# Attention scores of the second and third mixer as three products of high and low parts, with keys, queries and values projected in that order

## The reference

```python
def _diff_attention(dq, dk, dv, lam):
    s = jnp.einsum('bqhjd,bkhjd->bhjqk', dq, dk).astype(jnp.float32) * ATTN_SCALE
    p = jax.nn.softmax(s, axis=-1)
    a = (p[:, :, 0] - lam * p[:, :, 1]).astype(dv.dtype)
    return jnp.einsum('bhqk,bkhe->bqhe', a, dv)

def _gqa_attention(gq, gk, gv):
    s = jnp.einsum('bqhgd,bkhd->bhgqk', gq, gk).astype(jnp.float32) * ATTN_SCALE
    p = jax.nn.softmax(s, axis=-1).astype(gv.dtype)
    return jnp.einsum('bhgqk,bkhd->bqhgd', p, gv)
...
    dq, dk = _apply_rope(dq, cos, sin), _apply_rope(dk, cos, sin)
    gq, gk = _apply_rope(gq, cos, sin), _apply_rope(gk, cos, sin)
```

## Time and profile before

| | |
|---|---|
| median of three runs | 4403.17 us (4396.05 to 4407.77) |
| the profiled execution | 4407.63 us |
| its span | 4405.6 us |
| TensorE busy | 3956.6 us (90%) |
| VectorE, ScalarE, GpSimd busy | 2291.0, 1369.2, 1346.1 us |
| d of mix2, 1498 to 1616 us | granted clock 0.91 |
| g of mix2, 1838 to 1975 us | granted clock 0.99 |
| d of mix3, 3278 to 3372 us | granted clock 0.94 |
| g of mix3, 3538 to 3652 us | granted clock 0.97 |

### The profile page before, as it was taken

How to read it: one execution, slowest core, us unless ns; L and a number is a source line. 1 busy time by engine, 2 the same in 40 slices (tenths; PEclk the granted TensorE clock), 3 DMA queues, 4 the chain that set the end, 5 groups by cost and what they waited for, 6 DMA issues and landing times.

```text
span 4405.6 us, 50811 instructions
## 1 busy us (share of the span) xinstructions
PE 3956.6 (90%) x18628; PEld 3175.8 (72%) x18628; DVE 2291.0 (52%) x3495; ACT 1369.2 (31%) x1832; POOL 1346.1 (31%) x1012
## 2 busy tenths in 40 slices
PE   7999899989997979789879879999787989788999
PEld 6888676867776748558668768888674747577887
DVE  4676844146664361641682367777445353834334
ACT  3222633242224242252112331111424243225223
POOL 2444332434432103003222223322220303434443
PEclk8999999999998989899989989999998999899999
DMA  4454221233331102001111123332110201222222
GB/s 180 176 190 156 85 72 63 96 115 128 137 132 49 39 0 72 20 1 58 57 58 58 58 82 125 118 119 100 45 48 10 82 1 67 77 84 79 95 95 86
DMA packets 57219, 364.66 MB, mean 83 GB/s; under 512 B 5744, under 2 KB 12144, under 8 KB 13936
## 3 DMA queue, kind: packets, MB, share of 16 engines
q1 hardware_dynamic: 42064, 271.11, 17.5%
q10 hardware_dynamic: 15008, 91.49, 5.5%
HBM read 360.49 MB, written 2.10 MB: 82 GB/s over the span
## 4 chain that ended last, share of the span: by engine, by line
issue 66%; POOL 23%; PE 10%; DVE 0%; ACT 0%; POOLq 0%; DVEq 0%; ACTq 0%
POOL b_wlo L561 23%; PE ps L1647 3%; PE ps L1648 3%; PE ps L1649 3%; POOLq L575 0%; ACT ps L616 0%; DVE b_y L1156 0%; DVE b_x L1160 0%; PE ps L1699 0%; DVE b_y L1183 0%; PE ps L1710 0%; ACT b_whi L602 0%; POOLq L577 0%; DVE b_y L1209 0%; PE ps L1723 0%
## 5 line engine op out<-in xcount | busy, mean ns | idle before, releaser
L561 POOL TENSOR_TENSOR b_wlo<-b_raw,b_whi 128x512 fp32r<-128x512 f32 x1008 | 1345.9, 1366 | 3039.1 <-ACT b_whi L602 3039.1
L1647 PE MATMUL ps<-b_hhi,b_whi 128*128 128x512 f32 (+1 forms) x3160 | 1178.5, 373 | 69.5 <-DVE b_vp L1548 28.8
L1648 PE MATMUL ps<-b_hlo,b_whi 128*128 128x512 f32 (+1 forms) x3160 | 1163.3, 368 | 0.0
L1649 PE MATMUL ps<-b_hhi,b_wlo 128*128 128x512 f32 (+1 forms) x3160 | 1161.4, 368 | 0.0
L1647 PEld LDWEIGHTS ps<-b_hhi,b_whi 128*128 128x128 f32 x3160 | 603.5, 191 | 177.2 <-issue 57.3
L602 ACT ACTIVATE b_whi<-b_raw 128x2048 fp32r<-128x2048 f32 x252 | 480.7, 1908 | 752.4 <-PE ps L1649 744.9
L1648 PEld LDWEIGHTS ps<-b_hlo,b_whi 128*128 128x128 f32 x3160 | 603.7, 191 | 97.8 <-issue 2.2
L1649 PEld LDWEIGHTS ps<-b_hhi,b_wlo 128*128 128x128 f32 x3160 | 602.2, 191 | 99.1
L1104 DVE SCALAR_TENSOR_TENSOR b_macc<-b_mraw,b_csil,b_macc 128x256 f32<-128x256 f32 x868 | 506.0, 639 | 7.0
L1209 DVE TENSOR_TENSOR b_y<-ps,b_y 128x512 f32<-128x512 f32 x496 | 335.8, 689 | 274.7 <-PE ps L1649 274.7
L1647 PE MATMUL ps<-b_whi,b_dhi 128*128 128x512 f32 x992 | 399.7, 403 | 53.5 <-POOL b_wlo L561 29.0
(11 more groups left out here) (277 smaller groups left out, 4752.0 us busy)
## 6 DMA issues: line engine op xcount, KB each, us to landing
b_raw<-panels SPq DMA_DIRECT2D x252, 1024.0 KB, 4.8
b_mraw<-mod_panels ACTq DMA_DIRECT2D x78, 1024.0 KB, 6.7
b_y<-mod_panels ACTq DMA_DIRECT2D x3, 1024.0 KB, 15.9
b_xin<-xT SPq DMA_DIRECT2D x1, 2048.0 KB, 25.5
b_mraw<-mod_panels SPq DMA_DIRECT2D x2, 1024.0 KB, 19.0
b_rope<-rope ACTq DMA_DIRECT2D x4, 512.0 KB, 3.9
outT<-b_xout SPq DMA_DIRECT2D x4, 512.0 KB, 3.8
b_mod<-mod_panels ACTq DMA_DIRECT2D x1, 1024.0 KB, 20.9
```

Of the source, the lines that this page charges most:

```text
L561: ins = pool.tensor_tensor(wlo[:, s, c], raw[:, s, c], whi[:, s, c].bitcast(F32), ALU.subtract)
L1647: pe.matmul(out, a[0], b[0], start=first, stop=False)
L1648: pe.matmul(out, a[0], b[1], start=False, stop=False)
L1649: return pe.matmul(out, a[1], b[0], start=False, stop=last)
```

## The change

* Scores are three float32r products of high and low parts (`tri`), not one float32 product. Keys are split once: the high part by a Copy on ScalarE (`key_hi`), the low part by a subtraction on VectorE (`key_lo`). Queries are split at each unit's start: `query_hi` on ScalarE, `query_lo` on VectorE, in place of `masked_query`. The zeros of both parts are written by one memset and four copies.
* The factor 1/8 goes into the rotation of d's queries and the norm factor of g's.
* The panels of d come as keys, queries, values. Keys 0 to 2 are split before the queries' panels; key 3 after the value panels, into a slot of `whi` that is free then. The waits of TensorE ahead of the attention go: it waits for key and query at each unit and for the values before the first `weigh`.
* New tiles lie where others rest: `kh2` and `ql` on `gv` and `rope`, g's low queries in `wlo`, g's high key in `whi`.

```diff
-    ps = cols_panels(w, 0, 1024) + cols_panels(w, 1664, 2176) + merge(4480, v["w_br_diff_2"][l])
+    ps = cols_panels(w, 0, 512) + cols_panels(w, 1664, 2176) + cols_panels(w, 512, 1024) + merge(4480, v["w_br_diff_2"][l])
...
+            def key_hi(tag, t):
+
+                src = dk[:, t, :] if tag == "d" else gk[:, 0, :]
+                act.activation(split_keys(st, tag, t)[0], src, ACT.Copy).then_inc(*up("k_hi", X(tag, t)))
+
+            def query_hi(rows, r, j):
+
+                uno = rows.unit_no(r)
+                t, half, g = rows.unit(uno)
+                a, b = GROUPS[g]
+                prev = rows.last_row_with(uno, j)
+                if prev is not None:
+                    act.wait_ge(*at("scores", X(rows.tag, prev, j)))
+                else:
+                    act.wait_ge(*at("q_masks", X(rows.tag)))
+                act.wait_ge(*at(*rows.query_event(X, t, g)))
+                o = slice(64 * j, 64 * j + 64)
+                act.activation(split_query(st, rows.tag)[0][o, j, 0:b - a], aq[o, t, a:b], ACT.Copy).then_inc(*up("q_hi", X(rows.tag, uno, j)))
...
             def attention(rows):
                 for step in rows.first_steps():
                     row_exp(rows, *step)
                 for r in range(len(rows)):
                     steps = rows.next_steps(r)
+                    for q, j in steps:
+                        if rows.unit_start(q):
+                            query_hi(rows, q, j)
                     if rows.tag == "d" and steps:
                         row_exp(rows, *steps[0])
...
+            for t in range(3):
+                act.wait_ge(*at("ctx_kept", X("dk", t)))
+                key_hi("d", t)
...
+            act.wait_ge(panel_used, panel[0])
+            act.wait_ge(*at("ctx_kept", X("dk", 3)))
+            key_hi("d", 3)
             attention(rows)
...
+            def query_lo(rows, r, j):
...
+                dve.wait_ge(*at("q_hi", X(rows.tag, uno, j)))
+                dve.tensor_tensor(lo[o, j, 0:b - a], aq[o, t, a:b], hi[o, j, 0:b - a].bitcast(F32), ALU.subtract)\
+                   .then_inc(*up("q_lo", X(rows.tag, uno, j)))
-                dve.wait_ge(*at(*rows.query_event(X, t, g)))
-                dve.tensor_scalar(qm2[o, j, 0:b - a], aq[o, t, a:b], SCALE, None, ALU.mult).then_inc(*up("qm", X(rows.tag, uno, j)))
...
             def attention(rows):
-                for half in range(2):
-                    o = 64 * (1 - half)
-                    chain(dve.memset(qm2[o:o + 64, half, :], 0.0))
+                if rows.tag == "g":
+                    dve.wait_ge(panel_used, p0 + 15)
+                chain(dve.memset(pr2[:, 0, 1, 0:L], 0.0))
+                for part in split_query(st, rows.tag):
+                    for half in range(2):
+                        o = slice(64 * (1 - half), 64 * (1 - half) + 64)
+                        ins = dve.tensor_copy(part[o, half, :], pr2[o, 0, 1, 0:L])
+                ins.then_inc(*up("q_masks", X(rows.tag)))
...
                 for r in range(len(rows)):
                     steps = rows.next_steps(r)
                     for q, j in steps:
                         if rows.unit_start(q):
-                            masked_query(rows, q, j)
+                            query_lo(rows, q, j)
                     row_probs(rows, r)
                     for step in steps:
                         row_max(rows, *step)
...
-                if k0 == 0:
-                    pe.matmul(ps[:, b, :], q, keys(u)[:, 0:L], start=True, stop=True)
-                    ins = pe.matmul(ps[:, b + 1, 0:LC], q, keys(u)[:, L:TT], start=True, stop=True)
-                else:
-                    ins = pe.matmul(ps[:, b, 0:LC], q, keys(u)[:, L:TT], start=True, stop=True)
+                q = [part[:, j, (i % 4) * P:(i % 4 + 1) * P] for part in split_query(st, rows.tag)]
+                hi, lo = split_keys(st, rows.tag, u[0])
+                for n, (c0, c1) in enumerate(GROUPS if k0 == 0 else GROUPS[1:]):
+                    ins = tri(ps[:, b + n, 0:c1 - c0], q, (hi[:, c0:c1], lo[:, c0:c1]), True, True)
```

More of the change, by code:

```diff
@@ L373, in program @@
                 gk = sb("gk", [1, TT], F32, s3)
+            with ExitStack() as s3:
+                kh01 = sb("kh01", [2, TT], F32R, s3)
+            with ExitStack() as s3:
+                gkl = sb("gkl", [TT], F32R, s3)
         with ExitStack() as s2:
@@ L917, in keep_output @@
                 act.wait_ge(*at("pv", X(rows.tag, uno)))
-                act.wait_ge(*at("qm", X(rows.tag, uno, 1 if half is None else half)))
+                act.wait_ge(*at("q_lo", X(rows.tag, uno, 1 if half is None else half)))
                 act.activation(aq[o, t, a:b], ps[o, 6 + uno % 2, 0:b - a], ACT.Copy).then_inc(*up("kept", X(rows.tag, uno)))
@@ L969, in mix2 @@
                        .then_inc(*up("ctx_kept", X("dk", 2 * a + n)))
+            for t in range(3):
+                act.wait_ge(*at("ctx_kept", X("dk", t)))
+                key_hi("d", t)
+            for a in range(2):
+                next_split()
+                for n in range(2 if T > L else 0):
+                    act.wait_ge(*at("roped", X("dq", 2 * a + n)))
+                    act.activation(aq[:, 2 * a + n, L:TT], ps[:, 2 * (2 * a + n) % 4 + 1, 0:LC], ACT.Copy, scale=SCALE)\
+                       .then_inc(*up("ctx_kept", X("dq", 2 * a + n)))
+            rows = ROWS(st, "d")
+            first_queries(rows)
             for a in range(2):
@@ L1004, in mix2 @@
             rows = ROWS(st, "g")
+            act.wait_ge(panel_used, panel[0])
+            act.wait_ge(*at("roped", X("gk", 0)))
+            key_hi("g", 0)
+            first_queries(rows)
             attention(rows)
@@ L1503, in mix2 @@
             chain(dve.tensor_scalar(small[:, 48:49], small[:, 48:49], -lam_init, None, ALU.add))
+            chain(dve.tensor_scalar(small[:, 50:51], pcol("q_norm", l), SCALE, None, ALU.mult))
             chain(dve.tensor_scalar(small[:, 49:50], pcol("subln", l), 1.0 - lam_init, None, ALU.mult))
@@ L1507, in mix2 @@
                 turn("dk", t, ps[:, 2 * t % 4, :], dk[:, t, 0:L], pr2[:, 1, t % 2, 0:L], "rope")
+            for t in range(3):
+                key_lo("d", t)
             for t in range(4):
-                dve.wait_ge(*at("out", (p0 + 4 + t // 2, t % 2)))
-                turn("dq", t, ps[:, 2 * t % 4, :], aq[:, t, 0:L], pr2[:, 1, t % 2, 0:L], "rope")
+                dve.wait_ge(*at("out", (p0 + 2 + t // 2, t % 2)))
+                turn("dq", t, ps[:, 2 * t % 4, :], aq[:, t, 0:L], pr2[:, 1, t % 2, 0:L], "rope", SCALE)
             for t in range(4):
@@ L2050, in weigh, with attention @@
                 ins.then_inc(*up("pv", X(rows.tag, uno)))
-            def attention(rows, keys, values):
+            def attention(rows, values, last_value):
                 for step in rows.first_steps():
-                    row_scores(rows, *step, keys)
+                    row_scores(rows, *step)
                 for r in range(len(rows)):
                     for step in rows.next_steps(r):
-                        row_scores(rows, *step, keys)
+                        row_scores(rows, *step)
                     if r >= 1 and rows.unit_end(r - 1):
-                        weigh(rows, r - 1, values)
+                        weigh(rows, r - 1, values, last_value)
                     u, i, js, k0, k1 = rows[r]
@@ L2066, in attention @@
                     ins.then_inc(*up("tr", X(rows.tag, r)))
-                weigh(rows, len(rows) - 1, values)
+                weigh(rows, len(rows) - 1, values, last_value)
             for a in range(2):
```

88 lines of the change are left out of this document (54 added, 34 removed).

## The result

| | before | after |
|---|---|---|
| median | 4405.47 us (4396.05 to 4409.91) | 4531.14 us (4528.19 to 4533.94) |
| ratio, 95% interval | | 1.0283 (1.0269 to 1.0297) |
| span of the profiled execution | 4405.6 us | 4526.4 us |
| TensorE busy | 3956.6 us (90%) | 3980.8 us (88%) |
| granted clock, d of the second mixer (before 1498 to 1616, after 1500 to 1640 us) | 0.91 | 0.77 |

Slower, as forecast, but by 126 us and not by 67: the time lies outside the range given (4420 to 4520) and within 2 us of the clock rival's 4530, which had a chance of 0.12. Medians count every execution, but one of e7 (4471.78 us) and one of e9 (6204.65 us), both at a lower granted clock, are left out of the ratios.

What follows compares the result with a forecast made beforehand. TensorE was taken to nearly bound attention g, the score-to-transpose chain attention d. Terms -11 + 1.9 + 4.8 + 66 + 8 - 2 = +67 us on the profiled 4407.6 gave 4475, median about 4470, range 4420 to 4520.

Steps and rivals of the forecast that it cites:

- clock rival: Starts in g: the new gap drops the clock 22 times, 2.7 us each, 60 us, giving 4530; chance 0.12.
- part 6: Clock in d: larger gaps cost 1.5 us per pair or unit, some 8 us, within 0 and 25.
- Part 5: Unit starts inside attentions: the query's high part stands behind ScalarE's copy and exponential; +66 us, bounds 35 and 90.
- Part 1: Score steps: three float32r products take 1.05 us against 1.29 for float32; at most 33 us off.
- Part 2: Entry of d: with values last, TensorE's wait lies under the value panels; 5.6 us saved per mixer, 11 us.
- Part 3: Third mixer's query panels: the next panel's split stands behind three key copies on ScalarE; a stall of 1.9 us.
- Part 4: Entry of g: more mask copies and the query's two parts add 2.4 us, twice, 4.8 us.

Runs made afterwards that it cites:

- e7: e1 with the masked query written one iteration earlier on VectorE, behind the probabilities, in d for one of two heads; 4396.32 us, ratio 0.9964.
- e9: The changed kernel with both query parts written by VectorE, in g one iteration earlier behind the probabilities, in d at the unit's start; 4403.12 us, ratio 0.9988.
- e4: The changed kernel with unused filler products on TensorE before its wait for a new unit's query, 12 in g, 6 and 14 in d; 4480.21 us, ratio 1.0170.
- e10: e5 with unused filler products on TensorE before a unit's first scores, 8 in g, 4 and 10 in d; 4454.91 us, ratio 1.0110.
- e5: The kernel before, float32 scores kept, but ScalarE writes the masked query where the changed kernel makes the high part; 4493.54 us, ratio 1.0185.
- e2: The changed kernel with the query's high part on ScalarE one iteration earlier, before the copy of the transposed row; 4416.26 us, ratio 1.0018.
- e6: The changed kernel with both query parts made on VectorE at the place of the low part, none on ScalarE; 4413.39 us, ratio 1.0008.
- e1: The kernel before with only d's panels reordered to keys, queries, values and the wait for values moved to the first value product; 4397.31 us, ratio 0.9975.

## Why the prediction missed

**The step that failed is the clock's (part 6 and the clock rival's chance).** I priced it at 8 us, in d alone, and held against it in g that the earlier trace rows show full rate through a unit and that a value product of 5 us fills half of the time between two starts. The changed kernel has that value product and loses the clock all the same, at every start. The rows I took gave two ends: full rate behind a wait of 0.72 us, half rate behind one of 5.16 us. The forecast's own gap, some 3 us, lay between them, and I put it at the first end without saying so. The trace of the kernel before had rows for it in other stages, which I did not read. At 1793.16 us TensorE resumes behind 2.73 us of idleness and the clock falls, after 12 us at full clock (TensorE's timeline, then two windows in the columns told above):

```profile
1793.16 2.71 PE L2024 MATMUL ps<-b_pr,b_cst 128*128 128x512 f32 x4 [2.73 <-ACT b_pr L951]
1781.00:1793.20 12.20, 9.47 (x53) 7.68 (x51) 4.03 (x6) 2.20 (x3) 0.35 (x1) 1.00 0.23 86
1793.60:1796.80 3.20, 3.20 (x7) 1.95 (x6) 3.20 (x1) 0.00 (x0) 0.00 (x0) 0.50 0.00 0
```

e4 takes the gap away without an earlier start: 51 us. e10 does the same to e5: 39 us. Less the 8 us in the sum, the clock is 43 of the 54 us between the forecast's +67 and the span's +120.8. (Two slips in the recorded sum are small beside this: 6.5 starts at 1.5 us are 9.8 and not 8, and the terms as written add up to 67.7.) The price I gave the rival (2.7 us a start in g) was not right either: a start in the third mixer's g costs 1.3 us (17.2 against 15.95), a pair of the second mixer's g with two starts 2.5, and d pays as well, 1.2 a unit and 3.4 a pair. 7 x 1.3 + 7.5 x 2.5 + 3 x 1.2 + 3.5 x 3.4 = 43 us, of 48 between the two spans (4526.4 and 4478.4). The agreement of the rival's 4530 with the result is luck: it came out at the right total by a price too high for g and none for d beyond the 8 us.

The Trainium skill ("TensorE: Matmul & The Clock Gate", HAM oscillation) describes bursts that each start at half clock behind a recurring wait. The rows of g after the change agree in this: the clock is 0.50 behind the gap at six of six starts. They differ in that the first records still run at the full rate, for 0.5 to 1.1 us. I had weighed it below the rows of g before the change, which hold no such gap.

**Part 5, the unit's start: right.** Place, releaser and wait are as told, and e4 is the check of the numbers, since it has the late start without the clock: 15.95, 22.0, 26.2 and 35.4 us for the forecast 15.55, 21.0, 26.5 and 35.2. Its total, +73 us over before, is the forecast without its 8 us of clock (+59), to 14 us. e5 shows that the place alone does it: float32 scores and the kernel's old query, at the new place, give 10.2 us to the new unit's scores and a total of +84. e2 and e6 show the reverse: with the split kept and the place changed, +9 and +3.

**Part 1, the products: too cheap.** Between two sets of transposes a step takes 1.24 us (3710.93 to 3712.17), not 1.05: its first record takes 0.31 and not 0.23, its last 0.24 and not 0.12. Only the first of these is a price of the product. The transposes behind the last record reuse the banks out of which ScalarE copies the row before, and that copy (from 3711.21, 0.81 long) ends 0.15 us before they start; where it has long ended, as behind the filler of e4 (3658.49 to 3659.61), the step takes 1.12 us. The transposes ahead of it give 0.07 back (0.58 for 0.65). Scores and transposes of a row: 1.82 against 1.94, so 0.12 gained and not 0.24. The pitch of 0.23 was read in a row of equal products, with no copy to wait for. Over four rows this is about the 0.4 us by which the g unit of e4 exceeds the forecast, and over 128 steps, as an estimate, it would be most of those 14 us.

The Trainium skill ("FP8 and Floating Point Precision", TensorE Precision Notes) would by its four passes give a quarter, 0.32 of 1.29; the step in its real place gains 0.05 (0.17 where no copy holds it), and with the transposes 0.12. (The maximum by that rule is 128 x 0.32 + 32 x 0.11 = 45 us, not the 42 written.)

**Part 2, the entry of d: right.** From the last key kept to the third score step the kernel before takes 63.5 us in the third mixer (3219.87 to 3283.38), e1 57.5 (3214.83 to 3272.28): -6.1, forecast -5.6. In the changed kernel the first scores stand directly behind the last value product of the panel and at the full rate; TensorE's timeline, answering to the earlier trace rows:

```profile
3357.93 0.28 PE L1733 MATMUL ps<-b_whi,b_hlo 128*128 128x256 f32 x1
3358.05 0.39 PE L1731 MATMUL ps<-b_kh,b_qh 128*128 128x512 f32 x1
...
3362.39 0.48 PE L1731 MATMUL ps<-b_kh,b_qh 128*128 128x512 f32 x1 [2.11 <-ACT b_pr L931]
```

The third step is 4.3 us behind the end of the panels (forecast 4.6).

**Part 3, the stall: right in place, small in size.** The second query panel of the third mixer waits 3.02 us for its low parts (forecast 1.9), and e1, without the three key copies, 0.41. TensorE's timeline of the changed kernel, then of e1:

```profile
3311.00 0.80 PE L1731 MATMUL ps<-b_hhi,b_whi 128*128 128x512 f32 x1 [3.02 <-POOL b_wlo L584]
```

```profile
3223.09 0.50 PE L1647 MATMUL ps<-b_hhi,b_whi 128*128 128x512 f32 x1 [0.41 <-POOL b_wlo L561]
```

On ScalarE the three copies and the split stand one behind the other, as the working had it (TensorE's first record behind the stall is also at the lower rate, 0.80 for 0.50):

```profile
3300.12 0.39 ACT L1018 ACTIVATE b_dk<-ps 128x256 f32<-128x256 f32 x1 [7.95 <-DVE b_dk L1471]
3300.41 2.31 ACT L937 ACTIVATE b_kh<-b_dk 128x768 fp32r<-128x768 f32 x3
3302.61 1.90 ACT L625 ACTIVATE b_whi<-b_raw 128x2048 fp32r<-128x2048 f32 x1
```

**Part 4, the entry of g: right.** The wait is 17.17 us for 14.93, +2.2 for a forecast of +2.4:

```profile
3634.79 0.77 PE L1731 MATMUL ps<-b_whi,b_qh 128*128 128x512 f32 x1 [17.17 <-DVE b_wlo L1521]
```

**What stays open.** What decides whether a gap costs the clock is not known from these runs, and the length of the gap alone does not tell. In e6 the clock stays full behind gaps of 1.3 to 1.5 us in g and falls behind 2.08 us in d; in e5 it falls behind 2.29 us and stays full behind two of four gaps of 2.43. No run varied the gap alone. Nor did any run fill the gap of e6 in d, which would part the late start from the clock there.

## What to carry to other kernels

An instruction added to a chain is paid by what stands in front of it on its engine: 0.63 us of copy cost 2.2 us of waiting, and one line moved in the order took 115 us off. Then ask what the new gap does to TensorE's clock; if its length lies between a row that kept the clock and a row that lost it, look in the other stages of the same trace for a gap of that length; if there is none, both cases are open, and each gets its price and a real chance. Filler products in a gap tell late starts from a slow clock in one run. And read the pitch of a product among its real neighbours, not in a long row of its own kind, and ask of each record whether it is the work or a wait for a bank.

## What the runs showed of the hardware that I had not expected

* Behind one idle stretch of 3.20 us, after 8 us of nearly dense work, TensorE's granted clock was 0.50 for 3.2 us and then 0.99; the first records behind the gap still ran at the full rate (0.47 and 0.40 for the first two).
* Of seven starts of one kernel with gaps of 2.29 and 2.43 us, five lost the clock and two (2.43 us) did not (e5): 17.2 to 17.6 us a unit against 15.94.
* Useless products made the kernel 51 us faster (4531.1 to 4480.2).
* Behind float32 transposes the first record of a float32r step keeps TensorE 0.31 us, and 0.23 in a row of its own kind. A whole step takes 1.12 us, and 1.24 where the transposes behind it wait for a copy.
* A copy of 64x512 from float32 to float32r takes VectorE 0.42 us (e6) and ScalarE 0.63 us.
